# Moving 64 prompt tokens from the dense expert projection to gathered value rows

## What is computed

```python
def peer(h, wq, k1, k2, u, v):            # per token, 8 heads
    q = h @ wq
    s1, s2 = q_first @ k1.T, q_second @ k2.T          # 128 scores each
    v1, i1 = top_k(s1, 16); v2, i2 = top_k(s2, 16)
    cand = v1[..., :, None] + v2[..., None, :]        # 256 candidates
    sv, pos = top_k(cand, 16)                         # 16 experts per head
    idx = 128 * i1 + i2 at pos                        # of 16384 experts
    gate = softmax(sv)
    act = gelu(h . u[idx])
    return sum over 8 heads x 16 of gate * act * v[idx]
# then x = x + peer(...), and y = rmsnorm(x) * normf_g
```

## Time and profile before

| | |
|---|---|
| median of the runs | 2538.6 us |
| the profiled execution, its own time | 2536.08 us |
| its span in the trace | 2534.3 us |
| PE / weight loads / DVE / ACT / POOL busy | 95% / 88% / 60% / 33% / 38% |
| mean share of the granted TensorE clock | 0.972 |
| up tiles and gates, then down projection | up to 1806 us, then 1806 to 2514 us |
| moved by DMA | 454 MB, mean 179 GB/s |

### The profile page before, as it was taken

One profiled execution on the slowest core, in us unless ns is written; L12 is line 12 of the kernel. 1 busy time (PEld: TensorE's weight loads), 2 busy tenths in 40 slices (PEclk: granted clock), 3 DMA queues, 4 the chain that ended last, 5 costly groups with the idle time before them and its releaser, 6 DMA issues.

```text
span 2534.3 us, 42811 instructions
## 1 busy us (share of the span) xinstructions
PE 2405.4 (95%) x15412; PEld 2238.2 (88%) x15412; DVE 1525.3 (60%) x2837; ACT 838.7 (33%) x1534; POOL 963.6 (38%) x582
## 2 busy tenths in 40 slices
PE   6999899878998999999989999999999999999997
PEld 6899888877997999999989999999888888888885
DVE  7324624775765289998056767767565555555655
ACT  3212311562111011111146666666233232332322
POOL 4444320433553456666534444444421211111120
PEclk9999996988999999999989999999999999999998
DMA  7344434445663456633345445455888687777751
GB/s 233 119 138 150 145 126 146 131 131 176 198 182 116 133 180 206 204 132 129 127 143 185 177 170 180 173 183 186 267 257 259 217 263 219 250 229 241 244 159 62
DMA packets 315929, 454.00 MB, mean 179 GB/s; under 512 B 15680, under 2 KB 217536, under 8 KB 311504
## 3 DMA queue, kind: packets, MB, share of 16 engines
q1 hardware_dynamic: 185536, 256.47, 31.7%
q10 hardware_dynamic: 119056, 162.93, 19.0%
q0 software_dynamic: 11264, 33.60, 4.5%
HBM read 367.29 MB, written 152.72 MB: 205 GB/s over the span
## 4 chain that ended last, share of the span: by engine, by line
PE 82%; DVE 9%; ACT 4%; issue 2%; ACTq 1%; DMA 1%; POOL 0%; DVEq 0%; POOLq 0%
PE ps L469 47%; PE ps L726 27%; PE ps L699 2%; PE ps L610 1%; PE ps L659 1%; PE ps L602 1%; PE ps L555 1%; DVE rstd L1376 1%; DVE rr L1366 1%; DVE rstd L1365 0%; ACT oh L1013 0%; DVE rstd L1135 0%; ACT L849 0%; PE ps L642 0%; PE ps L580 0%
## 5 line engine op out<-in xcount | busy, mean ns | idle before, releaser
L415 POOL TENSOR_SCALAR w_hi<-w_raw 128x1024 fp32r<-128x1024 f32 x225 | 261.0, 1160 | 944.6 <-issue 703.0
L418 POOL TENSOR_TENSOR w_lo<-w_raw,w_hi 128x1024 fp32r<-128x1024 f32 x225 | 579.2, 2574 | 18.8
L469 PE MATMUL ps<-n_hi,w_hi 128*128 128x288 f32 x2048 | 437.8, 295 | 4.7 <-POOL w_lo L418 3.8
L469 PE MATMUL ps<-n_lo,w_hi 128*128 128x288 f32 x2048 | 438.2, 295 | 0.0
L469 PE MATMUL ps<-n_hi,w_lo 128*128 128x288 f32 x2048 | 437.6, 295 | 0.0
L726 PE MATMUL ps<-c_hi,w_lo 128*128 128x512 f32 x1024 | 403.4, 394 | 0.0
L726 PE MATMUL ps<-c_lo,w_hi 128*128 128x512 f32 x1024 | 401.4, 392 | 0.0
L726 PE MATMUL ps<-c_hi,w_hi 128*128 128x512 f32 x1024 | 397.6, 388 | 2.8 <-DVE w_lo L1629 2.1
L1629 DVE TENSOR_TENSOR w_lo<-w_raw,w_hi 128x1024 fp32r<-128x1024 f32 x127 | 155.6, 1226 | 306.1 <-ACT w_hi L1067 306.1
L469 PEld LDWEIGHTS ps<-n_hi,w_hi 128*128 128x128 f32 x2048 | 325.1, 188 | 6.4 <-POOL w_lo L418 5.0
L469 PEld LDWEIGHTS ps<-n_hi,w_lo 128*128 128x128 f32 x2048 | 329.5, 188 | 0.0
(11 more groups left out here) (267 smaller groups left out, 3625.9 us busy)
## 6 DMA issues: line engine op xcount, KB each, us to landing
value_rows<-in_down SPq DMA_DIRECT2D x128, 512.0 KB, 5.2
w_raw<-in_up SPq DMA_DIRECT2D x128, 512.0 KB, 3.4
w_raw<-in_down SPq DMA_DIRECT2D x128, 512.0 KB, 4.0
w_raw<-in_trunk SPq DMA_DIRECT2D x96, 512.0 KB, 3.4
act_scratch<-ast ACTq DMA_DIRECT2D x128, 288.0 KB, 2.1
c_act<-act_scratch ACTq DMA_DIRECT2D x16, 2048.0 KB, 11.5
gate_scratch<-gst ACTq DMA_DIRECT2D x32, 1024.0 KB, 4.3
c_gate<-gate_scratch ACTq DMA_DIRECT2D x15, 2048.0 KB, 20.5
```

The source lines that it names most:

```text
L415: nc.gpsimd.tensor_scalar(w_hi[j % 2][:, :, :], w_raw[j][:, :, :], 1.0, 1.0, ALU.mult, ALU.mult).then_inc(w_hi_done, 1)
L418: nc.gpsimd.tensor_tensor(w_lo[j % 2][:, :, :], w_raw[j][:, :, :], f(w_hi[j % 2][:, :, :]), ALU.subtract).then_inc(w_split, 1)
L469: last = nc.tensor.matmul(ps[:, 2 * p + a, 0:w], wt[:, k, :], act[:, k, t0 + a * w:t0 + (a + 1) * w], start=k == 0 and part == 0, stop=k = ...
```

## The change

It moves 64 prompt tokens, the last ones, from the dense side to the gathered side. `TD` is 448 now, `NS` is 128. With 128 gathered tokens each has a partition of its own, and a token's 128 picks are 128 steps (`PICKS` = 128) with `VB` = 6 buffers. The fold becomes a plain transpose of `v_sum` (eight of 128x128, after tile 6 of the last group). All dense operands have 448 columns, there are 28 gate blocks and so 56 gate tiles, and 68 plain tiles come first. The row numbers are worked out on 128 partitions; the three small DMAs that moved half of each table to other partitions (L1048), and ACT's wait for them (L1052), are gone. DVE's down loop over pairs of groups is written out, with 8 or 9 sums per group. At the end the squares of the dense tokens are taken block by block as the banks finish, those of the gathered tokens in one instruction.

```diff
-TD = SEQ
+TD = SEQ - NSEQ * DEC
 NS = TO - TD
-CD = TD // P
+CD = (TD + P - 1) // P
+DLAST = TD - (CD - 1) * P
-PICKS = PH * TOPK // 2
-VB = 4
+PICKS = PH * TOPK
+VB = 6
-LOOP1 = 60
+LOOP1 = 68
 LOOP2 = NGB // 2
...
@@ PE, last group
-                    if gg == 1 and d == 5:
+                    if gg == 1 and d == 6:
                         pe.wait_ge(v_summed, PICKS)
-                        pe.wait_ge(x_added, 1)
+                        pe.wait_ge(x_added, 2)
                         for e in range(KT):
-                            last = nc.tensor.matmul(ps[:, 0, e * NS:(e + 1) * NS], v_sum[:, e * P:(e + 1) * P],
-                                                    fold[:, :], start=True, stop=True)
+                            last = nc.tensor.transpose(ps[:, e // 4, (e % 4) * P:(e % 4 + 1) * P],
+                                                       v_sum[:, e * P:(e + 1) * P], idt[:, :])
                         last.then_inc(folded, 1)
@@ ACT
-            for dst, src in ((v_idx, full_u[3]), (a_idx, full_u[4]), (s_gate, full_f[3])):
-                act.dma_start(dst[NS:P, :], src[:, PICKS:2 * PICKS]).then_inc(table_in, 16)
             act.wait_ge(gparts_done, 3)
             for q in range(AHEAD - 1):
                 gated(q, q)
-            act.wait_ge(table_in, 16 * 3)
...
+            def dense_square(k):
+
+                act.wait_ge(x_added, k + 1)
+                act.wait_ge(sq_used, KT * 2 + k + (k == KT - 1))
+                A(sq[:, 0:TD], x[:, k, META:META + TD], ACT.Square).then_inc(sq_done, 1)
...
+            for j in range(KT - 1):
+                split_high((j + 1) % 4, (NGRP - 1) * KT + (N_D + 1 + j))
+                if j > 1:
+                    dense_square(j - 2)
+            dense_square(5)
+            dense_square(6)
+            act.wait_ge(s_added, 2)
+            A(sq_s[:, :, :], x[:, :, META + TD:], ACT.Square).then_inc(sq_done, 1)
+            dense_square(7)
+            mean_root(2)
@@ DVE
-                    if j >= 4:
-                        sums(j - 4)
+                    for _ in range(sums[j]):
+                        combine(next(picks))
+            def combine(m):
+
+                dve.wait_ge(v_in[m % VB], 16 * (m // VB + 1))
+                dve.wait_ge(s_act_in[m % VB], 16 * (m // VB + 1))
+                V.tensor_tensor(s_gate[:, m:m + 1], s_act[:, m:m + 1], s_gate[:, m:m + 1], ALU.mult
+                                ).then_inc(coef_done, 1)
+                dve.wait_ge(coef_done, m + 1)
+                if m:
+                    dve.wait_ge(v_summed, m)
+                V.scalar_tensor_tensor(v_sum[:, :], v_buf[m % VB][:, :], s_gate[:, m:m + 1], v_sum[:, :],
                                        ALU.mult, ALU.add).then_inc(v_summed, 1)
-            group(0, 0, 3, lambda q: combine(q, 0, PG))
-            with dve.Fori(0, NGRP // 2 - 1) as i:
-                for gg in range(2):
-                    group(1 - gg, i * 2 + (gg + 1), 0, lambda q: combine((gg + 1) * PG + q, i, 2 * PG))
+            group(0, 3, (0, 0, 1, 1, 0, 0, 0, 0))
+            for g in range(1, NGRP - 1):
+                group(g, 0, (1 + g % 2, 0, 0, 0, 1, 2, 2, 2))
...
             for q in range(KT - 1):
                 split_low((q + 1) % 4, (NGRP - 1) * KT + N_D + 1 + q)
-                if q < PG:
-                    combine((NGRP - 1) * PG + q, 0, PG)
...
+                combine(next(picks))
+                if q:
+                    add_down(q - 1)
+                if q > 1:
+                    dense_square(q - 2)
+            assert next(picks, None) is None
+            dense_square(5)
+            add_down(6)
             dve.wait_ge(folded, 1)
...
+            news = ps[:, 0:2, :].rearrange("p a (d t) -> p (a d) t", t=P)
+            for first, src in ((META + TD, news[:, :, DLAST:]), (META + SEQ, news[:, :, 0:DLAST])):
+                V.tensor_tensor(x[:, :, first:first + DLAST], x[:, :, first:first + DLAST], src, ALU.add
+                                ).then_inc(s_added, 1)
+            dense_square(6)
+            dve.wait_ge(sq_done, KT * 2 + 8)
+            V.tensor_reduce(ssum[:, TD:], sq_s[:, :, :].rearrange("p k t -> p t k"), AX, ALU.add).then_inc(sq_used, 1)
             add_down(7)
-            squares(2, 6)
-            squares(2, 7)
+            dense_square(7)
```

More of the change, by code:

```diff
@@ L780, in _, with norm @@
             epsc = small[:, 40:41]
-            def norm(r, raw, split=True):
+            def norm(r, raw):
                 t0 = META if r else 0
@@ L795, in norm, with mean_root @@
                     A(sq[:, t0:], x[:, k, t0:], ACT.Square).then_inc(sq_done, 1)
+                mean_root(r)
+                for k in range(KT):
+                    act.wait_ge(nrm_done, 8 * r + k + 1)
+                    A((n_hi if r else h_hi)[:, k, :], raw[:, k, :], ACT.Copy).then_inc(hi_done, 1)
+            def mean_root(r):
                 act.wait_ge(ms_done, r + 1)
-                A(halves(rstd[:, t0:]), opair(2) if r else pair(2), ACT.Sqrt, bias=epsc, scale=1.0 / D
+                A(halves(rstd[:, META if r else 0:]), opair(2) if r else pair(2), ACT.Sqrt, bias=epsc, scale=1.0 / D
                   ).then_inc(rms_done, 1)
-                if split:
-                    for k in range(KT):
-                        act.wait_ge(nrm_done, 8 * r + k + 1)
-                        A((n_hi if r else h_hi)[:, k, :], raw[:, k, :], ACT.Copy).then_inc(hi_done, 1)
             act.wait_ge(ones_set, 1)
@@ L1104, in _ @@
             group(1, NGRP - 3)
[L1105 to L1110 removed]
+            def dense_square(k):
+                act.wait_ge(x_added, k + 1)
+                act.wait_ge(sq_used, KT * 2 + k + (k == KT - 1))
+                A(sq[:, 0:TD], x[:, k, META:META + TD], ACT.Square).then_inc(sq_done, 1)
+            for j in range(KT):
+                split_high((j + 1) % 4, (NGRP - 2) * KT + (N_D + 1 + j))
+                if j < 4:
+                    c_split(1, NGRP - 1, (2 * j, 2 * j + 1))
+            for j in range(KT - 1):
[8 more added lines that the diff above has]
+            mean_root(2)
         @b.vector
@@ L1550, in _ @@
             dve.wait_ge(chosen_done, 1)
-            e1, e2, share = (chosen[0:NS, CT - 1, q, :] for q in range(3))
-            V.tensor_copy(full_u[0][:, :], e1)
-            link(V.tensor_tensor(full_f[0][:, 0:NS], idt[0:NS, 0:NS], iot[0:NS, 0:NS], ALU.mult))
-            V.tensor_reduce(s_col[:, :], full_f[0][:, 0:NS], AX, ALU.add)
+            e1, e2 = full_f[0], full_f[1]
+            for q, dst in enumerate((e1, e2, s_gate)):
+                V.tensor_copy(dst[0:DLAST, :], chosen[0:DLAST, CT - 1, q, :])
+                last = V.tensor_copy(dst[DLAST:P, :], chosen[DLAST:P, CT - 2, q, :])
@@ L1630, in split_low, with group @@
                                 ).then_inc(d_lo_done, 1)
-            def group(gg, g, first, sums):
+            def group(g, first, sums):
                 for j in range(KT):
@@ L1679, in _ @@
             for q in range(KT - 1):
                 split_low((q + 1) % 4, (NGRP - 1) * KT + N_D + 1 + q)
-                if q < PG:
-                    combine((NGRP - 1) * PG + q, 0, PG)
-                if q < PG and q < 1:
-                    add_down(q)
-            for q in range(1, PG):
-                add_down(q)
-            add_down(4)
-            dve.wait_ge(folded, 1)
-            V.tensor_tensor(x[:, :, META + TD:], x[:, :, META + TD:],
-                            ps[:, 0, :].rearrange("p (d t) -> p d t", t=NS), ALU.add).then_inc(x_added, 1)
@@ L1691, in _ @@
-            add_down(5)
-            for k in range(5):
-                squares(2, k)
-            add_down(6)
-            squares(2, 5)
+                combine(next(picks))
[6 more added lines that the diff above has]
+            add_down(6)
+            dve.wait_ge(folded, 1)
+            news = ps[:, 0:2, :].rearrange("p a (d t) -> p (a d) t", t=P)
```

107 lines of the change are left out of this document (51 added, 56 removed).

## The result

The changed kernel takes 2431.89 us (2430.7 to 2435.98, four runs) against 2537.63 us for the kernel before. The ratio is 0.9585, 95% interval 0.9569 to 0.9602: 105.7 us gained. The profiled execution took 2431.12 us, with a span of 2429.3; by its steps the prediction had 2440.6 there. The 9.5 us between the two are what the rest explains first.

What follows compares the result with a forecast made beforehand. PE, busy 95% of the span, was taken as the bound. Terms 83.2 + 9.7 + 0.3 - 0.65 + 0.4 + 2.5 = 95.5 us gave 2440.6 profiled; the median, 2.5 above, 2443; range 2435 to 2460 (own case 2436 to 2449).

Steps and rivals of the forecast that it cites:

- 3072 matmuls, 512 to 448 columns: Down projection: each matmul falls from 228.9 to 201.8 ns, gaining 83.2 us in all.
- gates and what is ahead of the down projection: Gate tiles: eight become plain ones, 9.7 us gained; ACT's wait for three table DMAs goes, 0.3 us gained.
- second down tile: Start of down projection: PE waits longer for ACT's last stores because the first tile is shorter, 0.65 us lost.
- fold to transposes: End of down projection: eight transposes replace the 1.7 us fold, gain 0.4 us (-0.2 to 0.7).
- last matmul to norm, and the norm: After the last down matmul: the wait before the norm falls from 4.9 to 2.4 us, gain 2.5 us.
- three prices: Down matmul savings: columns alone 81.9 us, straight line through 288 and 512 columns 84.5, time in proportion to columns 87.9.
- a line through measured points on both sides: Down matmuls: time falls 0.43 ns a column between 288 and 512 columns, 27.5 ns a matmul, 84.5 us.
- best ends: Whole kernel: the most favourable values of the terms (87.9, 2.5, 0.7) together give 2436 us.
- the 0.3 us for the three small DMAs: Where gates begin: ACT's 2.49 us wait for three table DMAs goes; 0.3 us gained, between 0 and 2.5.
- Rival 1: Down projection: DMA engines become the bound, 40.1 us a group in place of 38.7; 2464 us, chance 0.12.
- rivals 2 and 3: Down projection: DVE late in full tiles, 2453 us, chance 0.07; gathers run one after another, 2552 us, chance 0.03.
- rival 4: Down projection: matmuls don't get shorter (fixed time each), only 12 us gained, 2526 us; chance 0.01.

Runs made afterwards that it cites:

- widths run: Kernel before, down matmuls of a group's eight tiles cut to eight widths from 288 to 512 columns: 448 took 200.1 ns, 512 took 229.4 ns.
- before_free: Kernel before, with DVE raising the count that lets SP load the fifth down tile before making the fold matrix, not after: 2533.79 us (one run).
- the copies: Changed kernel with an extra 512 KB DMA copy to unused memory for every second down tile, or for every one: 2441.4 and 2534.7 us (one run each).

## Why the prediction missed its range

Against the profiled execution the sum came to 95.5 us, and 105.0 were gained. Term by term:

| term | forecast | measured | from |
|---|---|---|---|
| 3072 matmuls, 512 to 448 columns | 83.2 | 88.8 | 228.9 to 200.0 ns |
| gates and what is ahead of the down projection | 10.0 | 10.1 | first down matmul 1806.64 to 1796.54; 0.4 of it ahead of the first up tile |
| second down tile | -0.65 | +2.1 | the wait of 2.06 us gone |
| fold to transposes | 0.4 | 0.9 | gap in the down matmuls 1.9 to 1.0 us |
| last matmul to norm, and the norm | 2.5 | 3.2 | 4.87 to 2.36 us of wait (2.5), 1.95 to 1.24 us of matmuls (0.7) |

**The step that failed** is the term of the matmuls. The prediction named three prices, took one between the lowest two, and put proportion (87.9) at the far end; the truth was 0.9 beyond that end. It reasoned that a line through measured points on both sides is safe. (The line itself gave 84.5; the 83.2 taken lies 1.3 below it, and the reason given doesn't carry that step.) The widths run shows in its place that the time above the columns is 16.1 ns at 512 and 13.4 at 448, and goes up and down between. A matmul takes 200.0 ns where the prediction had 201.8: 1.8 ns for each of 3072 are 5.6 of the 9.5 us.

**The second step** was the wait before the second down tile. It was worked out as a fixed time on the clock, because it ends with a store, and the prediction then let the shorter first tile run into it. It didn't ask why that store took 4.5 us where others of its size take 2.1. The change removes the `link` behind the fold matrix (the diff of before_free above has the line); what it held back on DVE's queue (the count for SP, not only DVE's own work) wasn't followed. In place of -0.65 the term was +2.1, 2.7 us of the miss.

**A term that was missing** is the speed of the norm itself. Its four matmuls took 1.95 us before, at a mean granted clock of 0.60 behind a wait of 4.9 us, and 1.24 us after, at 1.00 behind 2.4 us: 0.7 us that stood in no sum.

**The range** was too narrow at its low end for these two. Its best ends gave 2436 with the median 2.5 us above the profile; the median was only 0.8 us above this profile, and the range ended at 2435.

**What held:** PE at full clock without a gap for the whole stage, DMA at 312 GB/s with PE not waiting (the "at most 20.6 us" for the loads of a group was a median, and the longest took 28.8 us after the change, still less than a group's 38.4), DVE fitting even in the full tiles, POOL still waiting mostly for sums, the way into the gates unchanged (6.2 and 3.7 us), 2.4 us to the norm. In the fullest run of tiles DVE is idle for 0.8 us each time, after two sums:

```profile
2020.42 1.28 DVE L1673 SCALAR_TENSOR_TENSOR v_sum<-v_buf,s_gate,v_sum 128x1024 f32<-128x1024 f32 x1
...
2023.89 1.23 DVE L1645 TENSOR_TENSOR w_lo<-w_raw,w_hi 128x1024 fp32r<-128x1024 f32 x1 [0.80 <-ACT w_hi L1069]
```

The gate term came out right as a sum, in part by luck. A gate tile's 7.58 us was taken as one price; it is 7.31 us of work and, once in four tiles, 1.05 us that comes from ACT's table loads. And the 0.3 us for the three small DMAs didn't show: the two tiles at the way into the gates took 30.46 us before and 30.54 after. What made up for it is the 0.4 us ahead of the first up tile.

**The rivals.** Rival 1 (DMA the bound) fell by the copies; rivals 2 and 3 by the waits list and by the run with half the gathers; rival 4 by the 200.0 ns.

## What to carry to other kernels

Where a sum multiplies one price by thousands, measure or bound that price beyond what the neighbours suggest: 1.8 ns a matmul was the larger part of the miss here. When a dependency is removed, follow every count that the waiting engine raises behind it, other engines' loads included. Look at the costliest loop for activation table loads: a loop entered with another function's table can pay for a change of table in every turn, and one small instruction before it can take that away.

## What was unexpected of the hardware

- The time of a matmul above its columns at 2.4 GHz is between 11.6 and 18.3 ns and not smooth in the width: 448 columns have 13.4 ns, 480 have 18.3, 512 have 16.1.
- Two table loads of 1.28 us in each turn of a loop of four tiles cost 1.05 us of PE time a turn, 12.6 us in 12 turns; the same loop needs none when a Gelu comes before it.
- With 8.5 gathers a group POOL spends 1.33 us on each indirect DMA (312.69 us for 236), with four a group 1.02 us (114.11 us for 112). It depends on what DVE does meanwhile. In the changed kernel those beside which DVE stands idle take 0.95 us, those beside which it is busy throughout 1.40 on average and up to 1.99. With half the gathers, 55 beside a low weight part alone take 0.94 us, and 14 beside a low part and a sum 1.55. Why is open. The kernel had room for it.
- The DMA engines held 364 GB/s with the mix of this stage and the copies, well under the 399 GB/s of stretches with large packets alone.
